# Four tiles at once behind each norm, and a fourth buffer for split weights, in a hybrid RWKV-7 / GLA / mLSTM trunk

## The reference, cut to what matters

```
x = LN(alpha*x + 0.5*(1+gate)*swiglu(x*(1+scale)+shift))     # ffn 0
proj = (x*(1+scale)+shift) @ w_in                              # 31 tiles of 128 outputs
mix  = concat(rwkv7(proj), gla(proj), mlstm(proj)) @ w_out
x = LN(alpha*x + (1+gate)*mix)
x = LN(alpha*x + 0.5*(1+gate)*swiglu(x*(1+scale)+shift))     # ffn 1
# shift, scale, gate: (silu(c) @ ada_w + ada_b), 9*1024 columns per layer
```

## Time and profile before

| | us |
|---|---|
| median of 3 runs (lowest, highest) | 1797.05 (1787.41, 1798.69) |
| the profiled execution, its own time | 1793.23 |
| its span, first to last instruction | 1791.4 |
| TensorE matmul busy | 1677.6 (94%) |
| VectorE, ScalarE, GpSimd busy | 971.3, 657.9, 171.9 |
| mean granted TensorE clock | 0.931 |

### The profile page before, as it was taken

The page is one execution under the profiler, slowest core; times in us unless marked ns, Lnnn a source line. Parts: engine busy times, 40 slices in busy tenths (PEclk is TensorE's granted clock), DMA queues, the critical chain, the costliest instruction groups (busy, mean ns, idle before and its releaser), DMA issues.

```text
span 1791.4 us, 32978 instructions
## 1 busy us (share of the span) xinstructions
PE 1677.6 (94%) x14132; PEld 1528.4 (85%) x14132; DVE 971.3 (54%) x1640; ACT 657.9 (37%) x947; POOL 171.9 (10%) x217
## 2 busy tenths in 40 slices
PE   4999999989899899999989999999898989899997
PEld 2899998979668678999989999989877777799997
DVE  1444446584644676545465445466846457655544
ACT  2233334463221235433353333355522124543333
POOL 1000012100300131000120000110030013200011
PEclk9999999999895599999999999999999568999998
DMA  9455654434551054444636555643332203644441
GB/s 335 167 205 212 200 198 155 151 105 139 169 172 39 3 193 166 153 153 148 217 118 212 189 188 174 224 144 135 106 107 85 68 1 98 238 144 151 153 150 69
DMA packets 92370, 270.23 MB, mean 151 GB/s; under 512 B 27169, under 2 KB 29505, under 8 KB 91969
## 3 DMA queue, kind: packets, MB, share of 16 engines
q1 hardware_dynamic: 87808, 265.50, 43.2%
q10 hardware_dynamic: 4416, 2.62, 0.6%
HBM read 261.83 MB, written 6.26 MB: 150 GB/s over the span
## 4 chain that ended last, share of the span: by engine, by line
PE 81%; DVE 12%; ACT 3%; DMA 2%; issue 2%; POOL 1%; ACTq 0%; DVEq 0%; SPq 0%; POOLq 0%
PE psV L1904 12%; PE psV L1905 12%; PE psV L1906 12%; PE psA L1904 9%; PE psA L1905 9%; PE psA L1906 9%; PE psV L705 3%; DMA raw<-weights_dram 2%; PE psC L1919 2%; DVE wlo L2191 2%; DVE PJ L1419 1%; ACT whi L2066 1%; PE psY L1919 1%; DVE ZT L2232 1%; PE psV L694 1%
## 5 line engine op out<-in xcount | busy, mean ns | idle before, releaser
L2191 DVE TENSOR_TENSOR wlo<-raw,whi 128x1024 fp32r<-128x1024 f32 x340 | 421.2, 1243 | 440.4 <-ACT whi L2066 437.7
L2066 ACT ACTIVATE whi<-raw 128x1024 fp32r<-128x1024 f32 x340 | 358.5, 1056 | 327.0 <-PE psV L1906 322.6
L1904 PE MATMUL psA<-XH,whi 128*128 128x320 f32 x1200 | 383.8, 320 | 29.5 <-DVE XL L2243 18.9
L1905 PE MATMUL psA<-XL,whi 128*128 128x320 f32 x1200 | 375.6, 313 | 0.0
L1906 PE MATMUL psA<-XH,wlo 128*128 128x320 f32 x1200 | 375.2, 313 | 0.0
L1904 PEld LDWEIGHTS psA<-XH,whi 128*128 128x128 f32 x1200 | 229.5, 191 | 50.4 <-issue 30.6
L1904 PE MATMUL psV<-XH,whi 128*128 128x320 f32 x816 | 260.2, 319 | 7.4 <-DVE wlo L2191 7.2
L1905 PE MATMUL psV<-XL,whi 128*128 128x320 f32 x816 | 255.4, 313 | 0.0
L1906 PE MATMUL psV<-XH,wlo 128*128 128x320 f32 x816 | 255.1, 313 | 0.0
L1905 PEld LDWEIGHTS psA<-XL,whi 128*128 128x128 f32 x1200 | 229.8, 191 | 0.3
L1906 PEld LDWEIGHTS psA<-XH,wlo 128*128 128x128 f32 x1200 | 229.6, 191 | 0.0
(11 more groups left out here) (383 smaller groups left out, 1870.6 us busy)
## 6 DMA issues: line engine op xcount, KB each, us to landing
raw<-weights_dram SPq DMA_DIRECT2D x450, 512.0 KB, 3.4
raw_own<-weights_dram SPq DMA_DIRECT2D x30, 512.0 KB, 5.8
raw<-weights_dram SPq DMA_DIRECT2D x8, 256.0 KB, 3.7
ZS<-st_rw_dram SPq DMA_DIRECT2D x2, 768.0 KB, 4.4
S<-st_gla_dram ACTq DMA_DIRECT2D x2, 768.0 KB, 4.5
o_glas_dram<-S SPq DMA_DIRECT2D x2, 768.0 KB
o_rws_dram<-ZS SPq DMA_DIRECT2D x2, 768.0 KB
CON<-consts_dram SPq DMA_DIRECT2D x1, 1288.5 KB, 10.0
```

Source lines behind the costliest of these rows:

```text
L1904: mm(out, whi[:, n % SPL, k], hi[:, kt], start=first, stop=False)
L1905: mm(out, whi[:, n % SPL, k], lo[:, kt], start=False, stop=False)
L2066: activation(whi[:, n % SPL], buffer(DENSE[n]), ACT.Copy).then_inc(hi_done, 1)
L2191: tt(wlo[:, n % SPL], buffer(DENSE[n]), whi[:, n % SPL].bitcast(F32), ALU.subtract).then_inc(lo_done, 1)
```

## The change

`LOCK` = 4 tiles begin together behind each of the five norms and at the entry, for up and for the projections (whose tiles 2 and 3 use `psV` banks). Within such a group, and in a tile alone, row blocks 0 to 5 go across the tiles and the last two (`LAST`) are taken tile by tile. The first chunk of each such group is split into a buffer pair of its own, `xhi` and `xlo`. To make room, two of the six own raw buffers now lie over `XH` or over the end of `HL`, with a wait on `ada_used` ahead of `modulate` where they lie over `XH`. In `streamed()` the dense chunks are issued ahead of an ada chunk as far as `seen + LOCK`.

```diff
+LOCK, LAST = 4, 2
@@ def streamed():
     for c in steps:
-        ahead = min(seen + SPL, len(split)) if seen else 0
+        ahead = min(seen + LOCK, len(split)) if seen else 0
         if not c[2] and seen < len(split) and first_out[split[seen]]:
             ahead = seen
@@
+LOCKED = [n for step, n in FIRST.items() if step[0] == "gate" and step[3] == 0 or step[0] == "proj" and step[2] == PROJ_ORDER[0]]
+SLOT, BEFORE, _ring, _last = [], [], 0, {}
+for _n in range(len(DENSE)):
+    SLOT.append(SPL if _n in LOCKED else _ring % SPL)
+    _ring += _n not in LOCKED
+    BEFORE.append(_last.get(SLOT[_n]))
+    _last[SLOT[_n]] = _n
@@
-        raw_own = ffn.take("raw_own", [P, AHEAD, 8, P])
+        xhi, xlo = ffn.take("xhi", [P, 8, P], F32R), ffn.take("xlo", [P, 8, P], F32R)
+        own = ffn.take("own", [P, AHEAD - 2, 8, P])
+        in_xh = nc.alloc_sbuf_tensor_at("in_xh", [P, 2, 8, P], F32, offset=xh_of_all)
+        in_hl = nc.alloc_sbuf_tensor_at("in_hl", [P, 2, 8, P], F32, offset=hl_end - 2 * 4 * 8 * P)
@@ def tiles(n0, banks, split_from=None):
                     pe.wait_ge(lo_done, n0 + len(banks))
-                    for kt in range(DT):
-                        if split_from is not None:
+                    places = [(kt, i) for kt in range(DT - LAST) for i in range(len(banks))]
+                    places += [(kt, i) for i in range(len(banks)) for kt in range(DT - LAST, DT)]
+                    for kt, i in places:
+                        if split_from is not None and i == 0:
                             pe.wait_ge(sem("x_split"), split_from + kt + 1)
-                        for i, bank in enumerate(banks):
-                            ins = three(bank[:, 0:TOK], n0 + i, kt, kt, kt == 0, kt == DT - 1, XH, XL)
+                        ins = three(banks[i][:, 0:TOK], n0 + i, kt, kt, kt == 0, kt == DT - 1, XH, XL)
@@ tensor, gate and proj
-                            tiles(n0, [open_up("gate", u), open_up("value", u), open_up("gate", u + 1)], (3 * L + 2 * s) * DT)
+                            tiles(n0, [open_up("gate", u), open_up("value", u), open_up("gate", u + 1), open_up("value", u + 1)],
+                                  (3 * L + 2 * s) * DT)
...
-                            for u in ((0, 1) if t == 0 else (t,)):
+                            for u in (range(LOCK) if q == 0 else (q,)):
+                                ring = bV if u in (2, 3) else bA
@@ scalar, split_to
-                        if n >= SPL:
-                            act.wait_ge(chunk_used, n - SPL + 1)
+                        if BEFORE[n] is not None:
+                            act.wait_ge(chunk_used, BEFORE[n] + 1)
@@ scalar and vector, modulate
+                    if after in IN_INPUT:
+                        act.wait_ge(ada_used, IN_INPUT[after])
@@ scalar, product
-                        split_to(n0 + ((d + 1) * kts - 1) // 8 + (2 if d < DT - 1 else 3))
+                        if d == DT - 1 and s % 3 == 1:
+                            act.wait_ge(*at("rw_zs", RP))
+                        split_to(n0 + ((d + 1) * kts - 1) // 8 + (2 if d < DT - 1 else LOCK))
@@ scalar and vector, enter
-                        split_to(2)
+                        split_to(LOCK - 1)
```

More of the change, by code:

```diff
@@ L264 @@
 RING = [[m for m, c in enumerate(LOADS) if c[3] == own] for own in (False, True)]
+GAPS = [n for n, step in enumerate(PLAN) if step[0] == "norm" and n + 1 < len(PLAN) and PLAN[n + 1][0] == "ada"]
+BEHIND_OUT = [k for k, n in enumerate(GAPS) if PLAN[n - 1][0] == "out"]
+IN_INPUT = {3 * PLAN[n][1] + PLAN[n][2]: sum(step[0] == "ada" for step in PLAN[:n]) + 2
+            for k, n in enumerate(GAPS) if k not in BEHIND_OUT}
 GROUPS = [step[1:4] for step in PLAN if step[0] == "ada" and step[4] == 0]
@@ L417, in hybrid_trunk @@
         FOLD = keep.take("FOLD", [P, 18])
+        xh_of_all = keep.at
         XH = keep.take("XH", [P, 9, TOK], F32R)
@@ L574, in landed, with split_hi, split_lo @@
         def landed(m):
-            own = LOADS[m][3]
-            q, n = RING[own].index(m), (RAW, AHEAD)[own]
-            return (loaded, loaded_own)[own][q % n], 16 * sum(1 + (LOADS[i][1] in HALVES) for i in RING[own][q % n:q + 1:n])
+            ring = LOADS[m][3]
+            q, n = RING[ring].index(m), (RAW, AHEAD)[ring]
+            return (loaded, loaded_own)[ring][q % n], 16 * sum(1 + (LOADS[i][1] in HALVES) for i in RING[ring][q % n:q + 1:n])
         def buffer(m):
-            own = LOADS[m][3]
-            return (raw, raw_own)[own][:, RING[own].index(m) % (RAW, AHEAD)[own]]
+            q = RING[LOADS[m][3]].index(m)
+            if not LOADS[m][3]:
+                return raw[:, q % RAW]
+            if q % AHEAD > 1:
+                return own[:, q % AHEAD - 2]
+            return (in_hl if q // AHEAD in BEHIND_OUT else in_xh)[:, q % AHEAD]
+        def split_hi(n):
+            return xhi[:] if SLOT[n] == SPL else whi[:, SLOT[n]]
+        def split_lo(n):
+            return xlo[:] if SLOT[n] == SPL else wlo[:, SLOT[n]]
         def product_end(d, kts):
@@ L1853, in mixer_states @@
                     sp.dma_start(N0[:].rearrange("p j s -> p (j s)"), of_layer(st_n)).then_inc(sem("ml_c00"), 16)
-                for m, (l, n, _, own) in enumerate(LOADS):
+                for m, (l, n, _, ring) in enumerate(LOADS):
                     if m == 4:
@@ L1871, in _ @@
                             rw_stores(sp)
-                    q, size = RING[own].index(m), (RAW, AHEAD)[own]
+                    q, size = RING[ring].index(m), (RAW, AHEAD)[ring]
                     if q >= size:
-                        last = RING[own][q - size]
+                        last = RING[ring][q - size]
                         if LOADS[last][2]:
@@ L1879, in _ @@
                     for L in range(DEPTH):
-                        if own and m == min((e for e in RING[True] if e > DENSE[FIRST["out", L]]), default=None):
+                        if ring and m == min((e for e in RING[True] if e > DENSE[FIRST["out", L]]), default=None):
                             now[0] = L
@@ L1888, in _ @@
                     else:
-                        sp.dma_start(whole(buffer(m)), weights[l, n]).then_inc((loaded, loaded_own)[own][q % size], 16)
+                        sp.dma_start(whole(buffer(m)), weights[l, n]).then_inc((loaded, loaded_own)[ring][q % size], 16)
                 for t in range(DT):
@@ L1902, in three @@
                 def three(out, n, k, kt, first, last, hi, lo):
-                    mm(out, whi[:, n % SPL, k], hi[:, kt], start=first, stop=False)
-                    mm(out, whi[:, n % SPL, k], lo[:, kt], start=False, stop=False)
-                    return mm(out, wlo[:, n % SPL, k], hi[:, kt], start=False, stop=last)
+                    mm(out, split_hi(n)[:, k], hi[:, kt], start=first, stop=False)
+                    mm(out, split_hi(n)[:, k], lo[:, kt], start=False, stop=False)
+                    return mm(out, split_lo(n)[:, k], hi[:, kt], start=False, stop=last)
                 def ada(a, group, q):
@@ L2037, in _ @@
                     elif kind == "proj":
-                        t = of[0]
-                        if t != 1:
+                        q = PROJ_AT[of[0]]
+                        if q == 0 or q >= LOCK:
                             banks = []
-                            for u in ((0, 1) if t == 0 else (t,)):
-                                banks.append(bA.open())
-                                bA.close(None, freed=at("proj_ready", PROJ_AT[u] + 1))
-                            tiles(n0, banks, (3 * L + 1) * DT if t == 0 else None)
+                            for u in (range(LOCK) if q == 0 else (q,)):
+                                ring = bV if u in (2, 3) else bA
+                                banks.append(ring.open())
+                                ring.close(None, freed=at("proj_ready", u + 1))
+                                if u in (2, 3):
+                                    proj_bank[L, u] = banks[-1]
+                            tiles(n0, banks, (3 * L + 1) * DT if q == 0 else None)
                     elif kind == "out":
@@ L2123, in _ @@
                         if n_next and n_next not in OUTS:
-                            split_to(n_next + 2)
+                            split_to(n_next + (2 if n_next not in LOCKED else LOCK - 1))
                         if of[2] == 3:
@@ L2190, in split_to @@
                         vec.wait_ge(hi_done, n + 1)
-                        tt(wlo[:, n % SPL], buffer(DENSE[n]), whi[:, n % SPL].bitcast(F32),
-                           ALU.subtract).then_inc(lo_done, 1)
+                        tt(split_lo(n), buffer(DENSE[n]), split_hi(n).bitcast(F32), ALU.subtract).then_inc(lo_done, 1)
                         nsplit[0] += 1
@@ L2229, in modulate @@
                     into_up = after is not None and s is not None and s % 3 != 1
+                    if after in IN_INPUT:
+                        vec.wait_ge(ada_used, IN_INPUT[after])
                     for t in range(DT + 1):
```

24 lines of the change are left out of this document (17 added, 7 removed).

## The result

The change made the kernel slower by 5.7%: 1893.31 us median of 4 runs (1888.72 to 1905.11) against 1792.99 for the kernel before (1787.41 to 1798.69, 4 runs), ratio 1.0569, 95% interval 1.0506 to 1.0633. The profiled execution took 1894.71 us. The direction was as predicted, the size was not: +100 us against +70, and 1893.31 lies just above the range.

What follows compares the result with a forecast made beforehand. TensorE, busy for 94% of the span, was taken to bound the kernel. Terms -12.3 + 68.8 + 3.8 + 10 = +70.3 us on the profiled 1793.23 gave 1863.5, adjusted to 1865 us; range 1836 to 1893.

Steps and rivals of the forecast that it cites:

- Part 1: Projections and ffn 1 up products, both layers: four tiles begun together keep TensorE from starving; four junctions sum to -12.3 us.
- Part 2: Buffers and waits: fourth split free behind down and out, 1.1 to 1.3 us at the entry; `ada_used` wait free.
- Part 3: Ffn 0 up products: ada loads released later, so TensorE waits +68.8 us; entry and layer 1's ffn 0 together +3.8.
- the twelve chunks that I counted: Layer 1, among ada chunks 97 to 111: each waits 2.9 to 3.0 us for its load, 35.8 us in all.
- The thirteen chunks that I counted: Layer 0, ada chunks from 19 on: eight wait 22.4 us together, five like chunk 23 wait 10.6 us together.
- Part 4: Low clock behind 27 new idle times of 2 to 3 us: +10 us, with bounds of 0 and 46.
- One in three of 27: Share of the new idle times followed by a low-clock stretch, each costing 1.7 us: 15 us, put down as +10.
- The bound of 46: Upper bound of the clock term: all 27 new idle times followed by a low stretch of 1.7 us.
- The case without waits: Ada chunks do not wait, since the extra dense load's split is done early enough: 1782 us, chance 0.08.
- The short waits: Ada waits come but landing is at its least and the clock stays up: +45 us, 1840 us, chance 0.12.
- The rival of the clock at every wait: Each of the 27 waits is followed by a low stretch: 46 instead of 10 us, 1901 us, chance 0.12.

Runs made afterwards that it cites:

- four_at_norms: Changed kernel with dense loads four ahead only where the next group is one of four, three ahead otherwise: 1786.25 us, ratio 0.9973 to the kernel before.
- last_none: four_at_norms with `LAST` = 0, all row blocks across the four tiles, none tile by tile at the end: 1799.1 us, ratio 1.0047 to the kernel before.
- early_wlo: four_at_norms with VectorE subtracting the next group's third chunk ahead of a product's last block: 1779.17 and, measured again, 1781.67 us; ratios 0.9945 and 0.9951 to the kernel before.
- order_only: Kernel before with one edit, dense loads issued four ahead of an ada load instead of three: 1909.66 us, ratio 1.066.
- old_order: Changed kernel with `seen + SPL` in place of `seen + LOCK`, dense loads three ahead as before: 1795.96 us, ratio 1.0041 to the kernel before.

## Why the prediction was right in direction and wrong in size

**Part 1, four tiles together: right.** In the changed kernel layer 0's projections begin at 357.45 and the fold stands at 371.61 (timeline of TensorE):

```profile
357.45 0.38 PE L1943 MATMUL psA<-XH,xhi 128*128 128x320 f32 x1 [3.03 <-DVE XL L2299]
```

```profile
371.61 0.63 PE L1968 MATMUL psV<-FOLD,MR 128*128 128x18 f32 x5
```

14.2 us for four tiles against 18.6. I had put 16: the low stretch of 1.7 us did not come here (clock 1.00 from 357 to 368), though it came at layer 1's projections (1288.2). The four groups that I summed took 18.6, 19.6, 18.6 and 17.7 us before and 14.2, 14.2, 15.7 and 14.2 now, 16.4 less. Their norms end 3.3 us later in all (Part 2), and the tile behind each group takes 2.1 us more. That leaves 11 us of gain against the 12.3 of my sum. The stretches that begin with these groups became 14 us shorter, but they hold the mixers too, whose lower clock moves a stretch by a few us from run to run: the one of layer 0 is 374.7 us before and 375.3 in four_at_norms, which has the same groups as the changed kernel. That taking the last row blocks tile by tile saves waits was right, last_none shows it.

**Part 2: one step wrong.** I wrote that the fourth split behind down and out "lies beside the last 3 us of matmuls, as the third did". That holds for ScalarE. On VectorE it went behind the last block, on the path of the norm: 2.35 us of subtractions instead of 1.22, and the first matmul 0.8 to 1.0 us later at each norm, 4.1 us in all. This is a part of why the waits for `XL` stayed at 19.2 us where I had about 10; the entry alone has 6.8. early_wlo took 2 to 5 us of it back. The wait on `ada_used` cost nothing, as predicted: early_wlo has it too, and there TensorE's waits at the first matmul behind the three norms that have it are 2.26, 2.63 and 2.26 us, the same as in the kernel before. The entry began 0.7 us later (43.68 against 43.03), not 1.1 to 1.3.

**Part 3, the order of the loads: right, and a term 7 us too small.** The step, what waits for what, and the 2.9 us per chunk hold. In layer 1 the twelve chunks that I counted are the ones that wait, 3.03 us at chunk 97 and 35.0 in all against 35.8; chunk 96 waited 3.4 in place of 1.7. In layer 0 it was 40.0 us more than before against 35.1. The thirteen chunks that I counted (those of `FILLED`) waited 31.0 us against 33.0, though the single ones differ: chunk 23, my example of its kind, waited 0.9 us and not 2.1, chunk 37 of the same kind 3.9. Five of the chunks to which I had given room waited 5.5 us, and chunk 17 at the start waited 3.6 us more than before in place of 2.1. All in all +79.7 us against 72.6.

**Part 4, the clock: the term that failed.** I put down 10 us, from "One in three of 27" and "Each low stretch costs 1.7 us". Both factors were too low. In layer 1, 12 of the 13 waits have a low stretch that begins during the wait or within about 1.6 us of its end, and eight of these are 6.8 us long, twice the one at 696.6 before. A window of the changed kernel over the first of them:

```profile
984.40:991.20 6.80, 4.89 (x22) 4.11 (x23) 2.51 (x7) 0.00 (x0) 0.00 (x0) 0.50 0.67 215
```

TensorE works for 4.9 us in it, at half the clock, which costs an estimated 2.4 us; in the one at 1021.9 it works for 6.3, which is 3.1 us. By TensorE's busy time the clock took 28.4 us in layer 1 and 10.2 in layer 0, 38.7 together, in place of 10. This 29 is nearly all of the 31 us by which the two profiled executions differ beyond my +70.3; 7 more are from part 3, and the smaller terms took some of that back. The bound of 46 held, but I had shut 25 as the upper end of the clock into the forecast's own range.

The "one in three" came from three idle times of 1.9 to 2.4 us, and the trace of before held others that I did not count. The idle times ahead of the groups at 306.79, 681.53, 925.54 and 1181.28, of 2.26, 1.84, 2.63 and 2.26 us, each have a low stretch, the first of them in the earlier trace rows. The other three:

```profile
682.90:686.40 3.50, 3.46 (x14) 3.27 (x13) 3.36 (x10) 2.21 (x5) 1.55 (x4) 0.51 0.17 68
...
925.30:928.70 3.40, 3.16 (x12) 3.19 (x13) 3.26 (x10) 2.46 (x5) 1.55 (x4) 0.50 0.38 153
...
1181.30:1184.70 3.40, 3.40 (x13) 3.19 (x13) 3.26 (x9) 2.29 (x4) 1.55 (x4) 0.50 0.01 5
```

With these, and one more of 1.95 us at 939.72 that has none, it is five of eight, not one of three. Ahead of those four TensorE also did the short matmuls of a norm, so they are not quite the case of a wait between tiles; but they spoke for a larger term.

**The rivals.** The case without waits fell: order_only is as slow as the changed kernel, old_order is not. The short waits fell too. The rival of the clock at every wait was nearly right in layer 1 (12 of 13). In layer 0 five of the 19 waits have a low stretch, all five among the ten waits of 2.4 us or more and none among the nine shorter ones. The rule of the Trainium skill that I set beside it (TensorE: Matmul & The Clock Gate, section "HAM oscillation") so agrees with the trace of layer 1 and with half of the longer waits of layer 0. The time measured, 1893, lies nearer to that rival's 1901 than to the forecast's 1865, and the clock's 38.7 us nearer to its 46 than to my 10. The estimate of 3.2 us per load, from the Trainium skill's page DMA: Bandwidth & Descriptors, section "Anatomy of one DMA", would have made the sum smaller; the changed kernel has 3.7 us from issue to landing at the median, from 984 to 1190:

```profile
DMA to landing us min/median/max: 3.1/3.7/4.9
```

**What stays open.** Why the lower clock follows 12 of 13 waits of about 3 us in layer 1 and only half of the waits of that length in layer 0 was not settled. Nor was the whole size of last_none. A fifth raw buffer, which might make four loads ahead harmless, was not tried.

## What to carry to other kernels

When a queue issues its loads in one written order, a constant in that order is a change of its own. Walk the ring for one load of each kind (who was in this buffer, when is it let go, how long is a landing) and compare the room with the room before; here a room of 5.4 us became 0.8 with nothing else to be seen in the code. When idle times of a few microseconds are put between stretches of matmuls, price the lower clock behind them from all idle times of that length that the trace has, or leave its whole bound in the range. And an instruction that is put at the end of a step stands at the head of the next one: on the engine of the norm one more subtraction of 1.2 us delayed five norms by 4.1 us.

## What the runs showed of the hardware

At waits of 2.4 to 3.4 us TensorE's granted clock fell to 0.5 in 12 of 13 cases in layer 1's first FFN; in layer 0's it fell at 5 of 10 waits of 2.4 to 5.2 us and at none of 9 shorter ones. The low stretches were 3.4 or 6.8 us long in both. In layer 1 they repeat with the distance of the waits (from 1021.9, 1035.6 and 1049.2, for waits that begin at 1019.6, 1033.1 and 1046.8). Matmuls of 256 columns into unused PSUM columns during the waits, whose results nobody reads, kept the clock at 1.00 behind all twelve filled waits of layer 1 and made that stretch 24.9 us shorter. With a start flag on these matmuls the kernel computed other results than without it.
